# Sixteen width classes of 8 columns in the expert loop, and a down projection of wide items in three half-precision products

## The reference, cut to what matters

```python
def expert_block(args):
    x_blk, e = args
    gu = x_blk @ w_gate_up[e] + b_gate_up[e]
    g = jnp.minimum(gu[:, :D_EXPERT], SWIGLU_LIMIT)
    u = jnp.clip(gu[:, D_EXPERT:], -SWIGLU_LIMIT, SWIGLU_LIMIT)
    act = (u + 1.0) * (g * jax.nn.sigmoid(SWIGLU_ALPHA * g))
    return act @ w_down[e] + b_down[e]
```

## Time and profile before

| what | us |
|---|---|
| median of 3 runs (range) | 2291.84 (2291.54 to 2293.78) |
| the profiled execution | 2293.2 |
| its span | 2291.4 |
| PE busy | 2031.7 |
| DVE busy | 1379.2 |
| ACT busy | 1041.5 |
| POOL busy | 323.0 |

### The profile page before, as it was taken

How to read it: one execution, slowest core, us unless ns; L and a number is a source line. 1 busy time by engine, 2 the same in 40 slices (tenths; PEclk the granted TensorE clock), 3 DMA queues, 4 the chain that set the end, 5 groups by cost and what they waited for, 6 DMA issues and landing times. The chain is left out here.

```text
span 2291.4 us, 50830 instructions
## 1 busy us (share of the span) xinstructions
PE 2031.7 (89%) x20529; PEld 1863.4 (81%) x20529; DVE 1379.2 (60%) x2605; ACT 1041.5 (45%) x1424; POOL 323.0 (14%) x296
## 2 busy tenths in 40 slices
PE   3889998999499559999999999999999999999940
PEld 2667886776278359999999999999999999998940
DVE  3477824455422755665556665775777776768645
ACT  4344211344411044444455555655656565656620
POOL 3000000000000031111111111211222222223220
PEclk9999978999599679999999999999999999999975
DMA  3111100001122557777887878889999999999938
GB/s 125 37 28 37 37 0 10 11 21 35 30 83 102 180 193 260 276 261 277 293 297 256 308 286 315 294 314 330 332 349 360 348 368 362 356 362 361 358 131 337
DMA packets 256760, 499.70 MB, mean 218 GB/s; under 512 B 17568, under 2 KB 38352, under 8 KB 256640
## 3 DMA queue, kind: packets, MB, share of 16 engines
q1 hardware_dynamic: 235264, 460.36, 56.1%
q0 software_dynamic: 20256, 33.93, 4.0%
q10 hardware_dynamic: 1152, 4.19, 0.5%
HBM read 487.93 MB, written 47.19 MB: 234 GB/s over the span
## 5 line engine op out<-in xcount | busy, mean ns | idle before, releaser
L1416 DVE SCALAR_TENSOR_TENSOR E_w_lo<-E_w_st,E_w_hi 128x2048 f16<-128x2048 f32 x260 | 594.5, 2286 | 61.7 <-ACT E_w_hi L1339 56.8
L1339 ACT ACTIVATE E_w_hi<-E_w_st 128x2048 f16<-128x2048 f32 x260 | 492.5, 1905 | 187.2 <-PE E_p_g L1578 93.3
L1586 PE MATMUL E_p_d<-E_a_f,E_w_st 128*128 128x160 f32 (+6 forms) x4096 | 530.9, 288 | 16.8 <-DVE E_a_f L1486 16.8
L1586 PEld LDWEIGHTS E_p_d<-E_a_f,E_w_st 128*128 128x128 f32 x4096 | 515.2, 191 | 25.0 <-issue 12.7
L1575 PE MATMUL E_p_g<-E_x_hi,E_w_hi 128*128 128x160 f16 (+6 forms) x2048 | 372.9, 224 | 4.9 <-issue 4.9
L1575 PE MATMUL E_p_u<-E_x_hi,E_w_hi 128*128 128x160 f16 (+6 forms) x2048 | 371.7, 223 | 5.1 <-DVE E_w_lo L1416 5.1
L1577 PE MATMUL E_p_g<-E_x_lo,E_w_hi 128*128 128x160 f16 (+6 forms) x2048 | 372.9, 224 | 0.0
L1578 PE MATMUL E_p_g<-E_x_hi,E_w_lo 128*128 128x160 f16 (+6 forms) x2048 | 372.9, 224 | 0.0
L1577 PE MATMUL E_p_u<-E_x_lo,E_w_hi 128*128 128x160 f16 (+6 forms) x2048 | 371.6, 223 | 0.0
L1578 PE MATMUL E_p_u<-E_x_hi,E_w_lo 128*128 128x160 f16 (+6 forms) x2048 | 371.6, 223 | 0.0
L1291 POOL DMA_INDIRECT expert_rows<-E_y_rows,E_idx_out x66 | 132.8, 2012 | 590.0 <-ACT E_y_rows L1357 579.4
(11 more groups left out here) (333 smaller groups left out, 3040.5 us busy)
## 6 DMA issues: line engine op xcount, KB each, us to landing
E_w_st<-in_w_gate_up SPq DMA_DIRECT2D x130, 2048.0 KB, 8.2
E_w_st<-in_w_down SPq DMA_DIRECT2D x64, 2048.0 KB, 14.6
F_part<-expert_rows SPq DMA_DIRECT2D x8, 2048.0 KB, 11.5
A_w_st<-in_w_in SPq DMA_DIRECT2D x20, 512.0 KB, 3.9
A_x_rows<-in_x SPq DMA_DIRECT2D x8, 512.0 KB, 8.2
B_wo_st<-in_w_out SPq DMA_DIRECT2D x8, 512.0 KB, 3.3
C_x_res<-in_x SPq DMA_DIRECT2D x8, 512.0 KB, 4.1
x_rows<-C_x SPq DMA_DIRECT2D x8, 512.0 KB, 4.9
```

The source lines that it names most:

```text
L1339: act.activation(w_hi[c % RI][:], staged(c % NG), ACT.Copy, scale=SW).then_inc(hi_s, 1)
L1416: dve.scalar_tensor_tensor(out=w_lo[c % RI][:], in0=staged(c % NG), scalar=SW, in1=w_hi[c % RI][:], op0=ALU.mult, op1=ALU.subtract, accum_ ...
L1586: ins = pe.matmul(banks[:, h, 0:w], staged(c)[:, k, h * P:(h + 1) * P], x[:, k, 0:w], start=h == 0 and k == 0, stop=k == KT - 1, skip_grou ...
```

## The change

**Widths.** There are sixteen classes, 8 columns apart, wide and narrow in turns: 256, 192, 184, 80, 176, 88, 168, 96, 160, 104, 152, 112, 144, 120, 136, 128. The next item can now be wider than the present one, so the body gets `w_next`, the widest class from this one on, and the row groups for the next item go by it. That is over 128 for all classes but the last.

**Down projection.** Items of 136 to 192 columns ("wide" below, `split` in the code) split their four down chunks too and do them as three float16 products. DVE's product goes back into `up`; ACT makes `a_hi` of it and DVE `a_lo`. The ring of four split buffers then runs over twelve chunks, and the next item's chunks 0 to 3 are split during the down projection instead of at c = 4 to 7.

**Smaller parts.** DVE writes the gate and up bias without waiting for the item before, and the down bias after c = 4. The sums in `fold` come at another place in wide items. SP runs by class; for wide items it loads the down slots when they have been split. Semaphores count 12 chunks an item. Stage D's tables are over 16 classes, with two comparisons instead of one.

```diff
-WIDTHS = (256, 192, 176, 160, 144, 128, 112, 96)
+WIDTHS = (256, 192, 184, 80, 176, 88, 168, 96, 160, 104, 152, 112, 144, 120, 136, 128)
+SPLIT = (136, 192)
...
+            step(dve.tensor_tensor(under[:], rem[:].unsqueeze(1).to_broadcast([P, NV, E_]),
+                                   below[:].unsqueeze(2).to_broadcast([P, NV, E_]), ALU.is_gt))
+            step(dve.tensor_tensor(kind[:], over[:], under[:], ALU.subtract))
...
-                        body(i, w)
+                        body(i, w, max(WIDTHS[v:]))
...
# ACT
+                    def act_hi(j):
+                        act.wait_ge(act_s, NP * i + j + 1)
+                        act.activation(a_hi[:, 2 * j:2 * j + 2, 0:w], up[j % 2][:, :, 0:w], ACT.Copy,
+                                       scale=SA / S1 / S1).then_inc(a_hi_s, 1)
...
                         act.wait_ge(gu_mm, NG * i + c + 1)
+                        if split and c == 7:
+                            act_hi(3)
                         if fast:
-                            split_hi(cc)
+                            if c + RI < chunks(w):
+                                split_own(c + RI)
+                            else:
+                                split_next(c + RI - NG)
+                        if split and c in (1, 3, 5):
+                            act_hi(c // 2)
...
-                    for g in range(2 * blocks(w)):
-                        x_part(i + 1, g, w)
+                    for g in range(2 if split else 2 * blocks(w_next)):
+                        x_part(i + 1, g, w_next)
                     for j in range(NP):
                         y_bias(j)
+                        if split:
+                            split_next(j)
+                            if j == 0:
+                                for g in range(2, 2 * blocks(w_next)):
+                                    x_part(i + 1, g, w_next)
...
# DVE
+                        if split and c == 7:
+                            act_lo(3)
...
                         if c % 2 == 0:
                             gate_times_sig(j)
+                        if split and c in (1, 3, 5):
+                            act_lo(j)
+                        if c == 4:
+                            bias_down()
...
# PE
+                    def down(c, k0=0, k1=KT):
...
+                            split_chunk(c, p_d[j % 2], a_hi, a_lo, k0, k1)
+                        else:
+                            whole_chunk(c, p_d[j % 2], a_f, k0, k1)
...
+                    down(8, 6, KT)
+                    for g in range(2, 2 * blocks(w_next)):
+                        turn_rows(i + 1, g, w_next, lambda: pe.wait_ge(x_out_s, NP * (i + 1) + g - 1))
+                    down(9, 6, KT)
```

More of the change, by code:

```diff
@@ L930, in stage_d @@
         base_full, jump, full_rows = (at(n, [P, E_], F32) for n in ("base_full", "jump", "full_rows"))
-        limit = at("limit", [P, NV + 1], F32)
-        over = at("over", [P, NV + 1, E_], F32)
+        above, below = at("above", [P, NV], F32), at("below", [P, NV], F32)
+        over, under = at("over", [P, NV, E_], F32), at("under", [P, NV, E_], F32)
+        last_no, loads = at("last_no", [1, 1], F32), at("loads", [1, NV], F32)
         kind, share, upto, start = (at(n, [P, NV, E_], F32) for n in ("kind", "share", "upto", "start"))
@@ L1031, in _ @@
             step(dve.tensor_copy(m.bounds[:], upto[0:1, :, E_ - 1]))
+            step(dve.tensor_scalar(last_no[:], upto[0:1, NV - 1, E_ - 1:E_], -1.0, None, ALU.add))
+            step(dve.tensor_scalar(loads[:], upto[0:1, :, E_ - 1], last_no[:, 0:1], None, ALU.min))
+            step(dve.tensor_copy(m.load_bounds[:], loads[:]))
             step(dve.tensor_tensor(start[:], upto[:], share[:], ALU.subtract))
@@ L1316, in run, with body @@
                 gather(1, 2)
[L1318 removed]
+                def body(i, w, w_next):
                     send(i)
@@ L1550, in turn_y @@
                     pe.wait_ge(yt_s, FREE + NP * i + j + 1)
-                    pe.wait_ge(x_out_s, NP * (i + 1) + x_step(w) * (2 * nb - 1 + j))
+                    pe.wait_ge(x_out_s, NP * (i + 1) + x_step(w_next) * (2 * blocks(w_next) - 1 + j))
                 else:
@@ L1565, in run, with body, split_chunk @@
                     turn_rows(0, g, CHUNK, lambda: pe.wait_ge(x_out_s, g - 1) if g >= 2 else None)
-                def body(i, w):
-                    def split_chunk(c, banks):
+                def body(i, w, w_next):
+                    split = chunks(w) == NC
+                    def split_chunk(c, banks, xh, xl, k0=0, k1=KT):
                         for h in range(2):
-                            for k in range(KT):
+                            for k in range(k0, k1):
                                 o_ = banks[:, h, 0:w]
@@ new lines, in body @@
+                        turn_rows(i + 1, g, w_next, lambda: pe.wait_ge(y_rows_s, FREE + NP * i + 1 + g))
+                    pe.wait_ge(a_s, NP * i + 3)
+                    down(8, 0, 6)
+                    down(9, 0, 6)
+                    pe.wait_ge(a_s, NP * i + 4)
+                    down(8, 6, KT)
+                    for g in range(2, 2 * blocks(w_next)):
+                        turn_rows(i + 1, g, w_next, lambda: pe.wait_ge(x_out_s, NP * (i + 1) + g - 1))
+                    down(9, 6, KT)
@@ L1630, in run @@
+                    for j in range(2, 4):
+                        down(NG + j)
+                        turn_y(i, j - 2, w, w_next)
                 by_class(pe, n_items, body)
-                turn_y(n_items, 2, CHUNK)
-                turn_y(n_items, 3, CHUNK)
+                turn_y(n_items, 2, CHUNK, CHUNK)
+                turn_y(n_items, 3, CHUNK, CHUNK)
                 if fast:
```

220 lines of the change are left out of this document (133 added, 87 removed).

## The result

The changed kernel takes **2382.9 us** (median of 4, 2376.5 to 2391.6) where the kernel before, on the same chip, takes 2292.8: a ratio of **1.0396**, 95% interval 1.0361 to 1.043. The forecast was 2352, 2312 to 2382. The direction was right, the size was not: the time lies 0.9 us outside the range. The profiled execution of the changed kernel took 2384.9 us with a span of 2383.1, 91.7 more than that of before.

A forecast was written before the change was run, and what follows sets the result against it. PE was taken to bound stage E, with DVE's chain limiting items of 144 columns and below. 2293.2 + 39.2 (-19.4 wide, +53.8 narrow, +4.8 stage D and start) + 21 clock - 1.4 = 2352 us, range 2312 to 2382.

The forecast's parts named there:

- The widths and what bounds them: Stage E: 16 wide and 16 narrow items; PE full in wide ones, DVE's chain limiting at 144 columns and below.
- The chain: DVE's work up to x_lo, before PE's third transposes: wide items only 19.4 us less of 81.3, narrow 53.8 more.
- The sum without the clock: Whole kernel at unchanged clock: -19.4 wide items, +53.8 narrow, +4.8 stage D and start, +39.2 us in all.
- The rule of the Trainium skill: Down products: about 81 ns per matmul, so 192 take at least 15.6 us, gaining nothing; rejected for the trace's 62.5 ns.
- The clock in the wide items: PE's waits of 3.2 to 3.8 us in ten wide items drop the clock, 2.1 us each: +21, bounds 0 and 25.
- The clock in the narrow items: PE's 2.0 us waits at the third transposes in 13 narrow items: no clock loss counted.
- a rival of 15%: The clock falls in narrow items too, 13 x 2.1 = 27 us more: 2379 us; chance 15%.
- Stage D: Class tables grow from 256 to 512 elements on DVE: 4.0 us more.
- The skip of one more class: Start of stage E: one more empty class to skip, 0.8 us more.
- the narrow-clock case: Upper end of the range: the clock falls in narrow items too, 2379 us; chance 15%.
- eight transposes at 1.3 us in 13 items: Narrow items, in the rival where PE stays the bound: transposes alone add 14.7 us, total 2226; 12% with its variants.

The follow-up runs named there:

- e9: The changed kernel with unused transposes filling PE's wait at the third transposes and, in items of 80, 88 and 96 columns, three further waits: 2333.1 us.
- e2: The changed kernel with the next item's x halves for the first two transpose groups made before the last weight split: 2292.5 us.
- e5: The changed kernel with early x halves, as in e2, and the wide items' down projection in one fp32 product again: 2313.1 us.
- e1: The changed kernel with only PE's wait at the third row transposes filled by unused transposes: 2349.8 us.
- e3: The changed kernel with the wide items' down projection in one fp32 product again, x halves still late: 2358.7 us.
- e4: The changed kernel with its 16 widths in descending order, three products kept in wide items: 2338.6 us.
- e6: The changed kernel with 15 descending classes (192 dropped), early x halves, and three products only from 152 columns on: 2279.4 us.
- e7: e6 plus unused transposes filling PE's waits at chunks seven, eight and the down projection in items of 80, 88 and 96 columns: 2242.6 us.
- e8: The kernel before with only the 16 classes of 8 columns, descending; one fp32 down product, late x halves: 2331.9 us.
- e10: The kernel before, its eight classes descending, plus early x halves and three down products from 160 columns on: 2266.0 us.

## Why the prediction missed, point by point

**The widths and what bounds them: right.** All windows of items fit the counts worked out from the reference.

**The chain: right.** The sum without the clock was 1371.1 - 19.4 + 53.8 = 1405.5 us for the items; the kernel with everything filled (e9) took 1400.6. In single items: 47.6 at 168 (forecast 47.95), third transposes at start + 36.8 (36.9). The products had the price that the rows gave, 62 ns each in the down projection too, here in the third item of 144 of e2, PE's timeline:

```profile
1866.92 0.23 PE L1690 MATMUL E_p_d<-E_a_lo,E_w_hi 128*128 128x144 f16 x1
1866.98 0.23 PE L1691 MATMUL E_p_d<-E_a_hi,E_w_lo 128*128 128x144 f16 x1
1867.05 0.23 PE L1688 MATMUL E_p_d<-E_a_hi,E_w_hi 128*128 128x144 f16 x1
```

The rule of the Trainium skill that the prediction weighed ("TensorE: Matmul & The Clock Gate", section "Back-to-back issue gap", about 81 ns at 128 columns) is not what happens here. At 168 columns the three products follow at 72 ns in e2, 13.9 us for 192 of them, and the fp32 records at 143 ns in e5, 18.2 us for 128: these are the 4 us by which the item became shorter.

**The clock in the wide items: right, in part by luck.** "I take 2.1 ..., ten times: +21": 22.7 in eleven items. But the way to the 2.1 was half of a stretch of 5.0 us or less. In the items of 144 and 136 the lower clock held for 6.8 us (as in the windows above), and each lost 2.1 to 2.6 us by it, not half.

**The clock in the narrow items: this step failed.** I wrote of the 2.0 us waits that 1.4 us at 96 had done nothing, and took zero for them, with 27 us in a rival of 15%. It was 21.5. At 104 and 112 that wait (1.9 us here) is the cause: filled, it gave back the clock, and with it the 7.5 us. The other 14.0 lie in the items of 80 and 88, and there it was not the wait alone: at 80 the clock fell with that wait filled (e1). What I should have looked at is everything TensorE waits for in such an item: at 80, it also stands 0.9, 1.5 and 1.7 us at the seventh and eighth chunk and before the down projection. I read the clock's fall as a matter of the longest single wait, and the rows of before could not bear that, since they held no item under 96 columns. Nor do the waits alone decide it: at 96 and 120 the same 1.9 us left the clock at 1.00 in the changed kernel, and in e3 it fell in an item of either width.

**Stage D: right** (3.8, forecast 4.0). **The skip of one more class: missed.** 0.8 forecast, 5.5 measured. I had no row for an empty class, and no run shows the 0.8; I took the price of a branch. The start of stage E in the profile, 4.9 us of "issue" ahead of PE's first matmul, held the bound: it stood there with one class skipped.

**Stages A to C: 5.4 us that no edit explains.** Their end falls at 757 or 758 us in the traces of before, e1, e4, e5, e6 and e9, and at 763 to 765 in those of the change, e2, e3, e7, e8 and e10; e6 and e7 have the same code there. It is a difference between executions, which I had not allowed for.

**The range and small slips.** The range is said to reach from 2331 - 16 = 2315 to the narrow-clock case, 2379; written down was 2312 to 2382. In the rivals, eight transposes at 1.3 us in 13 items are 16.9 us and not 14.7. Neither would have changed the outcome.

The sum again, in terms of the profiled executions: 2352 - 4.9 (chain) + 25.4 (clock: 46.4 for 21) + 4.7 (skip) - 0.2 (stage D) + 5.4 (A to C) + 1.1 (end) = 2383.5, against 2384.9 less the 1.4 that the profiled run of before stood over its median.

## What to carry to other kernels

Before a product is made cheaper, ask which step stands last in the queues that feed it. Here the x halves had to go ahead of one weight split, and the same edit turned from 24 us lost to 21 won. Where an engine's clock falls, a wait has a second price: it is worth a run with the wait filled by work that nobody reads, which tells that price apart from the chain's and may itself be a cheap cure. And two changes that are joined (a finer grid of widths, an order that alternates) should be summed apart: the grid was worth keeping only in the wide half, and the order not at all.

## What the runs showed of the hardware

- In items of 80 columns the granted clock was 0.71 in the mean although no single wait was over 1.7 us (e6), and 1.00 in the changed kernel's item of 96, which has one of 1.9.
- In e2 all three items of 80 kept the clock with waits of 0.9, 1.5 and 1.7 us at the seventh and eighth chunk and before the down projection. The window of the third:

```profile
977.70:1014.70 37.00, 32.21 (x543) 31.30 (x541) 27.11 (x61) 22.96 (x33) 8.53 (x7) 1.00 1.01 367
```

- The same code with the same waits can do either. In e5 the second and the third item of 80 both stand 0.9, 1.5 and 1.7 us at these places. The one kept the clock, the other lost it from the down projection's start for 13.7 us:

```profile
937.20:974.20 37.00, 32.22 (x542) 31.30 (x541) 26.94 (x61) 23.02 (x32) 8.53 (x7) 1.00 0.99 357
974.20:1016.90 42.70, 38.38 (x542) 37.73 (x541) 27.28 (x61) 23.02 (x32) 7.44 (x7) 0.84 1.01 366
```

  So neither the code of the item nor its list of waits decides alone. What does stays open.
- Once fallen, the lower clock held for 28 of an item's 48.2 us in e6, where 36.0 were enough with the wait filled (e7).
- Skipping an empty class body took about 5 us at the start of stage E. The instruction queues moved more packets there (4 and 3 or 4 for 2 and 1); whether the branch, the code's fetch or another engine's skip sets the 5 us was not tried.
